# Two transformer blocks on one core: token-tiled entries behind the branch norms, and 512-column products in the up and gate layers

## What is computed

```python
def squared_relu_mlp(x, w_up, w_down):          # first block, two layers, 4096 wide
    h = jax.nn.relu(x @ w_up)
    return (h * h) @ w_down

def swiglu(h, w_gate, w_up, w_down):            # second block, two layers, 2816 wide
    return (jax.nn.silu(h @ w_gate) * (h @ w_up)) @ w_down

for layer in range(DEPTH):                      # second block
    h = rms_norm_2(x, attn_pre_g[layer])
    y = mla_mixer(...) if layer < N_A_LAYERS else chunked_mixer(h, k_band, v_band, ...)
    x = x + rms_norm_2(y, attn_post_g[layer])
    h = rms_norm_2(x, ffn_pre_g[layer])
    f = swiglu(h, ffn_w_gate[layer], ffn_w_up[layer], ffn_w_down[layer])
    x = x + rms_norm_2(f, ffn_post_g[layer])
    if layer == N_A_LAYERS - 1:
        k_band, v_band = shared_kv(x, kv_src_g, w_kv_shared)
```

## Time and profile before

| | us |
|---|---|
| median of 3 runs (1159.13 to 1159.83) | 1159.61 |
| the profiled execution, its own time | 1158.01 |
| its span | 1156.2 |
| PE busy / DVE busy / ACT busy / POOL busy | 1113.8 / 676.5 / 532.0 / 43.1 |
| mean granted PE clock (1 is 2.4 GHz) | 0.995 |

### The profile page before, as it was taken

The page is one execution under the profiler, slowest core; times in us unless marked ns, Lnnn a source line. Parts: engine busy times, 40 slices in busy tenths (PEclk is TensorE's granted clock), DMA queues, the critical chain, the costliest instruction groups (busy, mean ns, idle before and its releaser), DMA issues.

```text
span 1156.2 us, 17758 instructions
## 1 busy us (share of the span) xinstructions
PE 1113.8 (96%) x7094; PEld 996.7 (86%) x7094; DVE 676.5 (59%) x941; ACT 532.0 (46%) x645; POOL 43.1 (4%) x71
## 2 busy tenths in 40 slices
PE   7999999999999999998999999999999979999997
PEld 6888899999889999988777999999798759999996
DVE  5756645454665454576667555454955766555554
ACT  5556434434344444345474433434534654334342
POOL 1000000000000000000000000001500410000000
PEclk9999999999999999999999999999999999999999
DMA  9843465555534555554432655556565143555650
GB/s 344 316 147 109 130 214 165 200 183 179 196 108 159 205 178 185 192 135 165 146 110 73 212 188 175 188 181 223 173 218 169 43 132 111 182 183 180 186 177 36
DMA packets 127273, 196.36 MB, mean 170 GB/s; under 512 B 6960, under 2 KB 97200, under 8 KB 127104
## 3 DMA queue, kind: packets, MB, share of 16 engines
q1 hardware_dynamic: 123872, 185.77, 49.0%
q0 software_dynamic: 3216, 9.51, 2.8%
q10 hardware_dynamic: 144, 0.52, 0.1%
HBM read 194.73 MB, written 1.05 MB: 169 GB/s over the span
## 4 chain that ended last, share of the span: by engine, by line
PE 85%; DVE 9%; ACT 3%; issue 1%; DMA 1%; DVEq 0%; SPq 0%; ACTq 0%
PE ps L1570 27%; PE ps L1572 26%; PE ps L1571 26%; DVE wlo L964 2%; DVE xs L1076 1%; ACT whi L611 1%; PE ps L1686 1%; DVE act_lo L1091 1%; DVE x L1122 1%; PE ps L2020 1%; DVE xs L1118 1%; DMA x<-x_in 1%; ACT junk L642 1%; PE ps L2018 1%; PE ps L1712 1%
## 5 line engine op out<-in xcount | busy, mean ns | idle before, releaser
L964 DVE TENSOR_TENSOR wlo<-raw,whi 128x2048 fp32r<-128x2048 f32 (+2 forms) x172 | 386.6, 2266 | 171.2 <-ACT whi L611 170.4
L1570 PE MATMUL ps<-act_hi,whi 128*128 128x256 f32 x1384 | 392.7, 284 | 6.2 <-DVE act_lo L1091 4.0
L1571 PE MATMUL ps<-act_lo,whi 128*128 128x256 f32 x1384 | 391.6, 283 | 0.0
L1572 PE MATMUL ps<-act_hi,wlo 128*128 128x256 f32 x1384 | 391.6, 283 | 0.0
L611 ACT ACTIVATE whi<-raw 128x2048 fp32r<-128x2048 f32 (+2 forms) x171 | 319.5, 1888 | 95.6 <-PE ps L1572 92.0
L1570 PEld LDWEIGHTS ps<-act_hi,whi 128*128 128x128 f32 x1384 | 263.6, 190 | 11.4 <-issue 7.6
L1571 PEld LDWEIGHTS ps<-act_lo,whi 128*128 128x128 f32 x1384 | 263.6, 190 | 2.0
L1572 PEld LDWEIGHTS ps<-act_hi,wlo 128*128 128x128 f32 x1384 | 263.6, 190 | 0.0
L1572 PE MATMUL ps<-whi,hlo 128*128 128x512 f32 x400 | 156.8, 392 | 0.0
L1571 PE MATMUL ps<-wlo,hhi 128*128 128x512 f32 x400 | 156.8, 392 | 0.0
L1570 PE MATMUL ps<-whi,hhi 128*128 128x512 f32 x400 | 156.2, 390 | 0.0
(11 more groups left out here) (186 smaller groups left out, 873.0 us busy)
## 6 DMA issues: line engine op xcount, KB each, us to landing
raw<-mlp_w_up_in SPq DMA_DIRECT2D x32, 1024.0 KB, 6.4
raw<-mlp_w_down_in SPq DMA_DIRECT2D x32, 1024.0 KB, 4.9
raw<-ffn_w_gate_in SPq DMA_DIRECT2D x22, 1024.0 KB, 5.3
raw<-ffn_w_up_in SPq DMA_DIRECT2D x22, 1024.0 KB, 5.3
raw<-ffn_w_down_in SPq DMA_DIRECT2D x22, 1024.0 KB, 4.8
raw<-attn_w_qkv_in SPq DMA_DIRECT2D x11, 1024.0 KB, 10.9
raw<-w_kv_shared_in SPq DMA_DIRECT2D x8, 1024.0 KB, 6.4
raw<-attn_w_o_in SPq DMA_DIRECT2D x4, 1024.0 KB, 5.1
```

The costliest lines, as they stand in the source:

```text
L964: nc.vector.tensor_tensor(wlo[:, s, 0:width], raw[:, s, 0:width], whi[:, s, 0:width].bitcast(F32), ALU.subtract).then_inc(lo_ready, 1)
L1570: nc.tensor.matmul(dst, lhsT=left[0], rhs=right[0], start=start, stop=False, **kw)
L1571: nc.tensor.matmul(dst, lhsT=left[0], rhs=right[1], start=False, stop=False, **kw)
L1572: return nc.tensor.matmul(dst, lhsT=left[1], rhs=right[0], start=False, stop=stop, **kw)
```

## The change

- **One act tensor** [P, KT, 2, T]: act_hi and act_lo of a k stand side by side, so that one matmul can take both as 512 columns.
- **wide_out** in place of tiles_out for the up, gate and key chunks: per weight tile one matmul `whi` by (act_hi, act_lo), 512 columns into a whole bank, and one `wlo` by act_hi, 256 columns into its first half. A chunk now fills two banks: 6 and 7 (GATE), 4 and 5 (UP); the squared-relu layers alternate between the pairs. The two halves of a bank must be summed: ACT copies the half with the act_lo part to SBUF (copy_rest), DVE adds the other (sum_gate, sum_up, sum_keys; in the squared-relu layers `square` adds and then does max(x, 0) * x in one instruction, in place of ACT's relu and DVE's square).
- **post_entry** in place of post for post0, fpost0 and post1: GpSimd multiplies beforehand x by the next norm's gains (premix_x) and the post gains by the next norm's gains (premix_rows). DVE multiplies the banks by both_rows and gets the next input with one instruction per quarter; ACT sums the squares by quarters (split_stats). x itself is updated later (update_x, three steps behind the first gate product), and the statistics, diagonals and the spread of the next norm's scale come later too: spread_scales stands after gate(1) instead of gate(0), for kvsrc after all four key chunks.
- **enter_by_tiles**: the first gate (or key) chunk runs token tile by token tile: per weight tile one matmul of 2 x 128 columns and one of 128, with the transposes of the second tile after the products of the first. The idle matmuls (BUSY) of the three places are dropped.
- The scaling of x by the final norm, `x_scaled`, moves from step 10 of the mla attention to step 7. The gain rows of kvsrc and pre1 are loaded later.

```diff
-        act_hi = sb("act_hi", [P, KT, T], F32R)
-        act_lo = sb("act_lo", [P, KT, T], F32R)
+        act = sb("act", [P, KT, 2, T], F32R)
+        act_hi = act[:, :, 0, :]
+        act_lo = act[:, :, 1, :]
...
+        up_sum = arena[:, 1536:2048]
+        y_gained = arena[:, 4096:6144].rearrange("p (t n) -> p t n", t=TT)
+        x_gained = {"fpre0": arena[:, 0:2048].rearrange("p (t n) -> p t n", t=TT), "kvsrc": xs, "fpre1": xs}
+        both_rows = {"fpre0": xs[:, 1, :], "kvsrc": arena[:, 7168:8192], "fpre1": arena[:, 7168:8192]}
...
+        GATE, UP = 6, 4
+        def turned_bank(name, p):
+            return 4 + (p % 2 if name in SPREAD else p)
...
+        def wide(b):
+            both = ps[:, b * HALF:(b + 2) * HALF].rearrange("p (f a t) -> p f a t", a=2, t=T)
+            return both[:, :, 0, :], both[:, :, 1, :]
...
+            def premix_x(then):
+                for t in range(TT):
+                    nc.gpsimd.tensor_tensor(x_gained[then][:, t, :], x[:, t, :], row(then), ALU.mult)\
+                        .then_inc(premixed, 1)
+            def premix_rows(name, then):
+                nc.gpsimd.tensor_tensor(both_rows[then], row(name), row(then), ALU.mult).then_inc(premixed, 1)
...
+            for name in ROWS[1:ROW["fpost0"] + 1]:
                 load_row(name)
+            wait_row(pool, "post0")
+            wait_row(pool, "fpre0")
+            pool.wait_ge(qr_turned, 2)
+            pool.wait_ge(x_scaled, 2)
+            premix_x("fpre0")
+            pool.wait_ge(mla.mixed, 8)
+            premix_rows("post0", "fpre0")
+            load_row("kvsrc")
+            load_row("pre1")
+            wait_row(pool, "fpost0")
+            wait_row(pool, "kvsrc")
+            pool.wait_ge(x_ready, 4 * XR["fpre0"] + 4)
+            pool.wait_ge(turned, 4 * TURN["fpre0"] + 4)
+            premix_x("kvsrc")
+            premix_rows("fpost0", "kvsrc")
...
+            wait_row(pool, "post1")
+            wait_row(pool, "fpre1")
+            pool.wait_ge(turned, 4 * TURN["pre1"] + 4)
+            premix_x("fpre1")
+            pool.wait_ge(chk.scored, KT)
+            premix_rows("post1", "fpre1")
...
+        def split_stats(act, sum_squares, root, name, done, acc):
+            for t in range(TT):
+                for h in range(2):
+                    p = 2 * t + h
+                    act.wait_ge(*((acc_part, 3 * acc + p + 1) if p < 3 else (w_used, done)))
+                    if p >= 2:
+                        act.wait_ge(squares, squares_before(name) + p - 1)
+                    sum_squares(name, t, bank(p), HALF, h)
+                root(name, t)
...
+                copy_turned(name, (0, 1))
+                hi_before(n0)
+                copy_turned(name, (2, 3))
+                copy_rest(gate, n0 + 1, GATE)
                 hi_before(n0 + 1)
                 assert cursor[0] == n0 + 4, (cursor[0], n0)
+                stats(name, rooted=False)
+                copy_rest(up_sum, n0 + 2, UP)
+                root(name, BOTH)
+                preload(ACT.Silu)
                 head(0, True)
...
+            def post_entry(name, before=None):
+                then, start = POSTS[name], squares_before(name)
+                i = list(POSTS).index(name)
+                def st(t, k, lo=0, hi=1):
+                    return norm_stat(name, t, k, lo, hi)
+                def factor(t):
+                    return norm_stat(before, t, 4) if before else 1.0 / D
+                def multiply(t, h):
+                    cols = slice(h * HALF, (h + 1) * HALF)
+                    nc.vector.tensor_tensor(y_gained[:, t, cols], bank(2 * t + h), both_rows[then][:, cols], ALU.mult)
+                def first_half(t):
+                    dve.wait_ge(squares, start + 2 * t + 1)
+                    link(nc.vector.tensor_scalar(st(t, 1, 1, 2), st(t, 0, 0, 1), factor(t), EPS, ALU.mult, ALU.add))
+                    multiply(t, 0)
+                def second_half(t):
+                    dve.wait_ge(squares, start + 2 * t + 2)
+                    nc.vector.scalar_tensor_tensor(out=st(t, 1), in0=st(t, 0, 1, 2), scalar=factor(t),
+                                                   in1=st(t, 1, 1, 2), op0=ALU.mult, op1=ALU.add)\
+                        .then_inc(var_ready, 1)
+                def newton(t):
+                    dve.wait_ge(root_ready, 2 * NORM[name] + t + 1)
+                    link(nc.vector.reciprocal(st(t, 3), st(t, 2)))
+                    link(nc.vector.scalar_tensor_tensor(out=st(t, 5), in0=st(t, 3), scalar=st(t, 1), in1=st(t, 3),
+                                                        op0=ALU.mult, op1=ALU.mult))
+                    link(nc.vector.tensor_scalar(st(t, 5), st(t, 5), -0.5, 1.5, ALU.mult, ALU.add))
+                    if before:
+                        link(nc.vector.scalar_tensor_tensor(out=st(t, 6), in0=st(t, 5),
+                                                            scalar=norm_stat(before, t, 6), in1=st(t, 3),
+                                                            op0=ALU.mult, op1=ALU.mult))
+                    else:
+                        link(nc.vector.tensor_tensor(st(t, 6), st(t, 5), st(t, 3), ALU.mult))
+                def next_input(t, h):
+                    cols = slice(h * HALF, (h + 1) * HALF)
+                    nc.vector.scalar_tensor_tensor(out=xs[:, t, cols], in0=y_gained[:, t, cols], scalar=st(t, 6),
+                                                   in1=x_gained[then][:, t, cols], op0=ALU.mult, op1=ALU.add)\
+                        .then_inc(xs_ready, 1)
+                dve.wait_ge(premixed, 3 * i + 3)
+                first_half(0)
+                second_half(0)
+                multiply(0, 1)
+                newton(0)
+                next_input(0, 0)
+                next_input(0, 1)
+                first_half(1)
+                second_half(1)
+                split_turned(then, (0,))
+                multiply(1, 1)
+                newton(1)
+                split_turned(then, (1,))
+                next_input(1, 0)
+                next_input(1, 1)
+                split_turned(then, (2, 3))
+            def update_x(name, t):
+                if t == 0:
+                    wait_row(dve, name)
+                for h in range(2):
+                    cols = slice(h * HALF, (h + 1) * HALF)
+                    ins = nc.vector.tensor_tensor(y_gained[:, t, cols], bank(2 * t + h), row(name)[:, cols], ALU.mult)
+                link(ins)
+                for h in range(2):
+                    cols = slice(h * HALF, (h + 1) * HALF)
+                    nc.vector.scalar_tensor_tensor(out=x[:, t, cols], in0=y_gained[:, t, cols],
+                                                   scalar=norm_stat(name, t, 6), in1=x[:, t, cols],
+                                                   op0=ALU.mult, op1=ALU.add).then_inc(x_ready, 1)
+                if t == TT - 1:
...
+                def square(i, b):
+                    dve.wait_ge(f.rest_copied, i + 1)
+                    nc.vector.tensor_tensor(by_token(up_sum), wide(b)[0], by_token(up_sum), ALU.add)\
+                        .then_inc(f.summed, 1)
+                    dve.wait_ge(f.summed, i + 1)
+                    nc.vector.scalar_tensor_tensor(out=hf, in0=up_sum, scalar=0.0, in1=up_sum, op0=ALU.max,
+                                                   op1=ALU.mult).then_inc(f.h_done, 1)
...
                 lo_before(n0)
+                update_x(post_name, 0)
+                sum_gate(0)
+                update_x(post_name, 1)
+                lo_before(n0 + 1)
+                diagonals(name)
+                sum_up(0)
                 copy_scales(name)
-                scale_gate(0, n0 + 1, True)
-                lo_before(n0 + 1)
-                gated(0, n0 + 2, True)
+                scale_gate(0)
+                gated(0, True)
                 hidden_lo(f, 0)
                 with dve.Fori(1, NF - 1) as i:
                     lo_part(SLOT[n0 + 4], W, i * 3 + (n0 + 2))
-                    scale_gate(i, i * 3 + n0)
...
+            def wide_out(w, b, enter=None):
+                for f in range(2):
+                    for k in range(KT):
+                        if enter and f == 0 and k % 4 == 0:
+                            wait_acts(enter, 3 + k // 4 if enter in BY_TILES else 2 + 2 * (k // 4))
+                        at = k * FC + f * P
+                        nc.tensor.matmul(bank(b + f), lhsT=w[0][:, at:at + P],
+                                         rhs=act[:, k, :, :].rearrange("p a t -> p (a t)"),
+                                         start=k == 0, stop=False, skip_group_check=True)
+                        ins = nc.tensor.matmul(bank(b + f, 0, T), lhsT=w[1][:, at:at + P], rhs=act_hi[:, k, :],
+                                               start=False, stop=k == KT - 1, skip_group_check=True)
...
+            def enter_by_tiles(name, w, b):
+                turn(name, parts=(0, 1))
+                for t in range(TT):
```

(63 more changed lines are left out.)

189 lines of the change are left out of this document (108 added, 81 removed).

## The result

The changed kernel takes 1168.7 us (median of 4 runs, 1167.5 to 1171.5), the kernel before 1159.5 beside it: a ratio of 1.0077, 95% interval 1.0061 to 1.0093. It is slower, by 9.2 us, where 8.2 less were forecast, and it lies outside the range. The profiled execution took 1167.50, its span 1165.7, 9.5 more than that of before; 0.5 of that arose before mlp0 (its first transposes stand at 121.47 instead of 120.95), which leaves 9.0 for the change.

The account below looks back on a forecast made before the run. The prediction took PE, busy 96% of the span, as the bound. From the profiled 1158.0 us, -13.3 (wide products) + 1.3 (layer ends) + 3.8 (entries) gave 1149.8, plus 1.6 for the median 1151.4; whole range 1146.5 to 1163.8.

Parts of the forecast that it names:

- I count 0: GpSimd's premix multiplies at the entries: 3.4 us per 1024 columns, premix_rows in time, nearly no interference with DVE; 0 us.
- Rival (d): At two entries: GpSimd and DVE exclude each other or premix_rows is late, 2 x 2.7 or so; 1157 us, chance 0.06.
- R: At each of the three entries behind a branch norm: the moment the last product before it ends on PE.
- Part 1: Wide up, gate and key chunks: 0.173 us less PE time each, 77 chunks, 13.3 us gained.
- Part 3: Entries at post0, fpost0 and post1, queues replayed: 1.5, 0.9 and 1.4 us lost, together 3.8.
- rival (a): Short 128-token second matmuls in each entry are slow, 0.229 us each; 1163.7 us in all, chance 0.25.
- (b): Wide products: the pairs save nothing because weight loads set the pace; 1164.7 us, chance 0.06.
- The clock in part 3: Low clock for most of tile 0 in the entries: 1.5 us lost at post0, 0.7 at kvsrc, 0.6 at post1.
- 2.1 us of waiting inside tile 0: First entry: waiting said to take up part of the 3.8 us that the low clock adds, leaving 1.5.
- part 2: Layer ends, where DVE is late: 0.85 us at mix1, 0.4 at pre0 (1.3 lost), and 2.0 at kvsrc, paid in the entries.

Follow-up runs that it names:

- e4: Only the wide products in all 80 chunks, with the entries, idle matmuls and post norms of the kernel before and no GpSimd multiply; 1152.2 us, 0.9941.
- e1: Changed kernel with each of GpSimd's nine multiplies handling 1 of 1024 columns (wrong results), all else kept; 1157.6 us, 0.9983 to the kernel before.
- e8: e5 with 4, 13 and 11 idle matmuls before the entries' transposes, 2 before first products, fpost0's multiplies in mid-ffn0; 1144.5 us, 0.9865.
- e2: Changed kernel with GpSimd's 1024-column multiplies cut into eight of 128 columns each; 1158.2 us, 0.9992 to the kernel before.
- e10: e8 with GpSimd's multiplies whole again (1024 columns); 1149.2 us, 0.9917 to the kernel before.
- e3: Changed kernel with whole multiplies moved: early in the mla attention, mid-ffn0, and before the chunked attention; 1158.6 us, 0.9994 to the kernel before.
- e5: e2 with the split of down(0)'s chunk taken out of the loop and put before silu; 1154.2 us, 0.9942 to the kernel before.
- e9: e2 with 4, 13 and 11 idle matmuls before the entries' transposes, 2 before first products, 4 before down(0); 1151.4 us, 0.9922.
- e6: e2 with 17, 48 and 42 idle matmuls before the entries' transposes, 8 before first products, 16 before down(0); 1196.4 us, 1.0307.
- e7: e5 with 17, 48 and 42 idle matmuls before the entries' transposes, 8 before first products, fpost0's multiplies in mid-ffn0; 1181.0 us, 1.0184.

## Why the prediction was wrong

The sum was -13.3 + 1.3 + 3.8 with nothing for GpSimd. Sorted by what the runs can separate, with the start before mlp0 taken out: wide products with the late ends (2.0 at kvsrc among them) forecast -10.0, measured -8.6 (e4 to before, by profile); the new entries without GpSimd's work +1.8, measured +6.7 (e1 to e4; 5.4 by the medians); GpSimd 0, measured +10.9 (after to e1). The misses are 1.4, 4.9 and 10.9, together the 17.2 us between -8.2 and +9.0.

- **"I count 0", GpSimd beside DVE: this step failed, and it alone turned the sign.** "By that the four multiplies should have lost up to 1 us each; the trace does not bear it out" was read from means. In the earlier trace rows the 0.72 us of DVE's multiplies is the mean of 0.67, 0.88, 0.68 and 0.88, and six of GpSimd's eight instructions take 0.85 to 0.87, two 1.37 and 1.33 (the kernel before):

```profile
831.59 1.37 POOL L501 TENSOR_SCALAR arena<-arena 128x256 f32<-128x256 f32 x1
832.17 0.88 DVE L1076 TENSOR_TENSOR xs<-x,rows 128x512 f32<-128x512 f32 x1
```

  So each engine did hold off the other, by 0.2 and 0.5 us. DVE's small instructions in the same stretch show it too (POOL, then DVE, the kernel before):

```profile
829.71 0.85 POOL L501 TENSOR_SCALAR arena<-arena 128x256 f32<-128x256 f32 x1
829.78 0.34 DVE L1018 TENSOR_TENSOR stat<-stat 128x2 f32<-128x2 f32 x1
830.15 0.16 DVE L1019 TENSOR_TENSOR stat<-stat 128x2 f32<-128x2 f32 x1
830.35 0.23 DVE L1020 TENSOR_SCALAR stat<-stat 128x2 f32<-128x2 f32 x1
```

  The first takes twice its usual 0.16 us. But the second runs its 0.16 while GpSimd's instruction still lasts, so these rows show the mechanism and not the size that it would have beside a multiply of 1024 columns. That size was set by the length of one GpSimd multiply and by the place: what is hit is not DVE's load but a chain of small steps on PE's path. The rule of the Trainium skill (SBUF — State Buffer, Who interferes with whom), an exclusive lock for a whole instruction, fits the multiplies of the changed kernel: the DVE instructions of 2 columns beside them end within 0.03 us of their ends. It does not fit GpSimd's TENSOR_SCALAR above as it is recorded: a DVE instruction with two SBUF inputs ran undisturbed within its 0.85 us (spans of GpSimd are rough in this profile). The price that the Trainium skill has for the multiply (an estimate of 2.3 us by GPSIMD Engine Reference, Elementwise) was right: 2.33 to 2.43 us measured where DVE was not in its way, where I took 3.4 from another operation. premix_rows was not late, as forecast.
- Rival (d) named this mechanism with 0.06 and 1157, priced as 2.7 us at two entries. By the table (after minus e1) it costs 1.6 in the mla attention, 4.8 between R and gate(2) in ffn0, where three multiplies meet the diagonals, and 4.5 in the chunked attention: 10.9. At the entries themselves, where I had looked, it costs nothing. The 4.8 are less than the stall of 4.5 and the 2.0 that up(1) loses, since the wait before down(0) and the low clock behind it, 3.5 us in e1, are then gone.
- **Part 1**: the direction was right. The pair is 0.353 us in mlp0, not 0.349; against 5.76 that leaves 0.11 of 0.173 a chunk, 0.137 in the swiglu layers, about 10 us in all instead of 13.3. The ends cost less than the 3.3 forecast: 0.7 at mix1 (0.85), 0.3 (0.4), about 1.6 at kvsrc (2.0).
- **Part 3, the replay of the queues** was close: first products at R + 5.0 (5.4), gate(0) done at R + 17.3 (16.9 with the clock's 1.5), the wait before down(0) 1.8 in e1 and at post1 of the changed kernel (2.1). The 128-column matmul keeps the pace taken: the 32 matmuls of tile 1, of both kinds, in 3.74 us (627.60 to 631.34), 0.117 each, so rival (a), which had 0.25, is false, and so is (b).
- **The clock in part 3** was mis-sized, and that is most of the 4.9. Tile 0 takes 6.4 to 6.5 us in all three entries of the changed kernel and 3.8 at full clock: 2.6 each, where I took 1.5, 0.6 and 0.7. (In e1 it takes 5.8, 6.4 and 5.4, with the same instructions.) The working took part of the doubled tile back for "2.1 us of waiting inside tile 0", but its own replay has the first half done at 7.3 and the second ready at 7.6, a wait of 0.3; in e8 tile 0 takes 3.9 us, with hardly any. And a term was missing: behind the wait before down(0) the clock is low as well, which costs 1.7 us in each swiglu layer of e1 (7.0 instead of 5.3). Against that PE does not wait before gate(2) there, forecast 0.7 each. Against e4 the entries of e1 cost 2.4 at post0 (forecast 1.5), 0.7 at kvsrc (forecast a gain of 1.1 once the 2.0 of part 2 is taken out) and 2.7 at post1 (1.4). Another 0.7 lies in the rest of ffn0, where e2, with the same entries, has 155.7 us and the changed kernel 156.7: that is not shown to be theirs. In e8, where idle matmuls fill the first wait and the one before down(0) is gone, the three stretches are 2.7, 1.9 and 2.0 shorter than in e4. The kernel before had idle matmuls there; I named their absence and gave it too little.

## What to carry to other kernels

Work given to GpSimd is not free because GpSimd is idle: ask which small DVE instructions stand on the critical path while it runs. If there are any, cut it into pieces or put it where DVE has slack. When PE has to wait, the wait also costs what the low clock takes from the work behind it; put idle matmuls there, sized from a measured row, or reorder the queue that PE waits for. A change with several parts should be tried part by part: here the wide products were worth 7 us, the new entries 7.6 once mended, and the multiplies on GpSimd cost 11.

## What the hardware showed

- A GpSimd multiply of 128x1024 with SBUF inputs takes 2.3 to 2.4 us, and held off DVE's TENSOR_TENSOR from SBUF (0.16 became 2.33) and its fp32 TENSOR_SCALAR from SBUF (0.17 became 2.27), but not the RECIPROCAL beside it (0.15 at 597.47 and 942.89) nor instructions that read PSUM (0.42 and 0.41 us at 937.78 and 939.62). This agrees with the section of the Trainium skill named above. In the earlier trace rows a GpSimd TENSOR_SCALAR of 128x256 (0.85 us) held off such a DVE instruction by 0.2 us at most. The other way round, two multiplies beside DVE's weight splits in the middle of ffn0 took 6.80 us instead of 4.72 (e10):

```profile
686.44 6.80 POOL L579 TENSOR_TENSOR xs<-x,rows 128x1024 f32<-128x1024 f32 x2 [53.52 <-DVE hlo L1370]
```

- Cut in eight, a multiply of 1024 columns costs GpSimd some 3.4 us instead of 2.4 (a piece every 0.42 us at 637 in e2), and the kernel is faster. The 9.0 us for sixteen pieces hold one of 2.57 us, beside a weight split of DVE's.
- The clock also fell where nothing had been changed. At the start of the mla attention the profiled executions of e3, e5, e8 and e9 ran some 6 us at the low level, those of before, after, e1, e2, e4, e6, e7 and e10 did not, with the same instructions on PE; that is 3 us of the 103.6 and 103.7 in the table. Windows of e8 and of e2:

```profile
564.00:566.00 2.00, 2.00 (x4) 0.81 (x4) 0.00 (x0) 0.74 (x4) 0.00 (x0) 0.50 1.00 406
```

```profile
564.00:566.00 2.00, 2.00 (x14) 1.65 (x14) 1.17 (x8) 1.08 (x5) 0.00 (x0) 1.00 0.98 401
```

  What decides it stays open. Executions of one kernel differ in their mean clock by as much: of e8's four, the two with a mean of 0.998 took 1143.3 and 1143.7 us, the two with 0.995, the profiled one among them, 1145.4 and 1146.2.
- An fp32 matmul of 256 columns is listed as two records and takes 0.44 us; the fp32r one of 256 columns takes 0.12.
